# Expert weights of a hybrid block as 2 MB transfers with 16 KB rows, and the contraction orders permuted to fit

## The reference

```
logits = xt @ w_router + b_router                       # 512 tokens, 32 experts
top_val, top_idx = lax.top_k(logits, 4)
gates = jax.nn.softmax(top_val, axis=-1)
...
gu = xb @ w_gate_up[e] + b_gate_up[e]                   # (1024) x (1024 x 2048)
gate = jnp.minimum(gu[:, :D_EXPERT], 7.0)
up = jnp.clip(gu[:, D_EXPERT:], -7.0, 7.0)
act = (up + 1.0) * gate * jax.nn.sigmoid(1.702 * gate)
yb = act @ w_down[e] + b_down[e]                        # (1024) x (1024 x 1024)
```

## Time and profile before

| | |
|---|---|
| median of 3 runs | 1363.3 us (1361.44 to 1363.33) |
| profiled execution, its own time | 1363.13 us |
| its span, first to last instruction | 1361.4 us |
| PE busy | 1264.2 us, 93% |
| DVE, ACT, POOL busy | 38%, 21%, 12% |
| DMA moved | 455.66 MB, mean 335 GB/s |
| ring<-in_w_gate_up_dram | 256 transfers of 1024 KB |
| ring<-in_w_down_dram | 128 transfers of 1024 KB |
| mean granted TensorE clock | 0.969 of full speed |

### The profile page before, as it was taken

One profiled execution on the slowest core, in us unless ns is written; L12 is line 12 of the kernel. 1 busy time (PEld: TensorE's weight loads), 2 busy tenths in 40 slices (PEclk: granted clock), 3 DMA queues, 4 the chain that ended last, 5 costly groups with the idle time before them and its releaser, 6 DMA issues.

```text
span 1361.4 us, 52741 instructions
## 1 busy us (share of the span) xinstructions
PE 1264.2 (93%) x21755; PEld 742.5 (55%) x21755; DVE 520.2 (38%) x1710; ACT 288.4 (21%) x500; POOL 162.0 (12%) x257
## 2 busy tenths in 40 slices
PE   8999999973998999999999999999999999998882
PEld 4546555431655656656555655555565556555451
DVE  6553233226333333333333333343333334332238
ACT  4521124041121221121122121112212212211112
POOL 4100320033010010100101010010100101000010
PEclk9999999985999999999999999999999999999896
DMA  7452151237299999999999999999999999999997
GB/s 238 143 194 91 32 197 46 114 148 302 77 417 418 406 418 406 418 397 418 404 405 417 399 417 408 417 406 417 409 418 403 417 398 404 417 417 418 417 421 282
DMA packets 96851, 455.66 MB, mean 335 GB/s; under 512 B 11033, under 2 KB 22986, under 8 KB 63466
## 3 DMA queue, kind: packets, MB, share of 16 engines
q1 hardware_dynamic: 92768, 445.69, 81.5%
q0 software_dynamic: 3888, 8.40, 1.7%
q10 hardware_dynamic: 90, 0.03, 0.0%
HBM read 432.52 MB, written 23.27 MB: 335 GB/s over the span
## 4 chain that ended last, share of the span: by engine, by line
PE 65%; DMA 30%; DVE 3%; issue 2%; SPq 0%; POOL 0%; ACT 0%; DVEq 0%; POOLq 0%; ACTq 0%
PE ps L1696 25%; DMA ring<-in_w_gate_up_dram 18%; PE ps L1717 12%; PE ps L1309 11%; DMA ring<-in_w_down_dram 10%; PE ps L1658 5%; PE ps L1329 4%; PE ps L1376 1%; DMA x_rows_dram<-cat,rowi 1%; PE ps L1689 1%; PE ps L1708 1%; PE ps L1667 1%; PE ps L1369 1%; PE ps L1338 0%; DMA ring<-x_rows_dram 0%
## 5 line engine op out<-in xcount | busy, mean ns | idle before, releaser
L1696 PE MATMUL ps<-ring,cat 128*32 128x256 f32 x9856 | 557.7, 384 | 15.3 <-DMA ring<-in_w_gate_up_dram 15.3
L1696 PEld LDWEIGHTS ps<-ring,cat 128*32 128x32 f32 x9856 | 308.4, 111 | 236.0 <-DMA ring<-in_w_gate_up_dram 20.1
L1717 PE MATMUL ps<-ring,cat 128*32 128x256 f32 x4928 | 281.5, 379 | 3.9 <-DMA ring<-in_w_down_dram 3.0
L1717 PEld LDWEIGHTS ps<-ring,cat 128*32 128x32 f32 x4928 | 146.0, 110 | 110.5 <-DMA ring<-in_w_down_dram 7.5
L1309 PE MATMUL ps<-hbuf,ring 128*128 128x512 f32 x320 | 147.5, 607 | 0.4 <-DVE hbuf L846 0.4
L778 ACT ACTIVATE cat<-cat 128x128 f32<-128x128 f32 x154 | 47.7, 310 | 453.9 <-DVE cat L1239 453.9
L559 POOL DMA_INDIRECT pair_rows_dram<-cat,rowi x75 | 74.7, 996 | 505.1 <-ACT cat L782 505.1
L1221 DVE TENSOR_REDUCE wslot<-ps 128x2 f32<-128x6 f32 x77 | 12.7, 165 | 317.1 <-ACT cat L782 316.6
L782 ACT ACTIVATE cat<-ps,wslot 128x256 f32<-128x256 f32 x77 | 36.5, 474 | 367.7 <-PE ps L1717 363.0
L1658 PE MATMUL ps<-hbuf,cat 128*32 128x256 bf16 x2496 | 108.7, 274 | 3.7 <-DVE cat L1204 3.7
L1239 DVE TENSOR_SCALAR cat<-ps 128x128 f32<-128x128 f32 x154 | 44.9, 292 | 166.7 <-PE ps L1696 165.2
(11 more groups left out here) (308 smaller groups left out, 816.7 us busy)
## 6 DMA issues: line engine op xcount, KB each, us to landing
ring<-in_w_gate_up_dram SPq DMA_DIRECT2D x256, 1024.0 KB
ring<-in_w_down_dram SPq DMA_DIRECT2D x128, 1024.0 KB
ring<-in_w_in_dram SPq DMA_DIRECT2D x10, 1024.0 KB, 6.3
pair_rows_dram<-cat SPq DMA_DIRECT2D x4, 2048.0 KB, 11.0
ring<-pair_rows_dram SPq DMA_DIRECT2D x4, 2048.0 KB, 20.5
ring<-in_w_out_dram SPq DMA_DIRECT2D x1, 4096.0 KB, 12.9
ring<-in_x_dram SPq DMA_DIRECT2D x4, 512.0 KB, 5.4
x_rows_dram<-ring SPq DMA_DIRECT2D x1, 2048.0 KB, 16.9
```

The lines of the kernel that those rows point to most:

```text
L1696: last = mm(ps[SLOTS * q:SLOTS * (q + 1), gu_bank(half), 0:2 * P].rearrange("p (s j i) -> p s j i", s=2, j=4), xgT[:, SLOTS * u:SLOTS * (u ...
L1717: last = mm(ps[SLOTS * q:SLOTS * (q + 1), 1, 0:QD], actT[:, c // 4, SLOTS * (c % 4):SLOTS * (c % 4 + 1)], w[:, i, q * QD:(q + 1) * QD], st ...
```

## The change

The loads of `refill` are joined in pairs. Two neighbouring units, now "a pair", come with one transfer of 2 MiB in which each partition receives 16 KB from 16 KB that lie together in DRAM. For gate/up that is two neighbouring rows of 8 KB, for down four neighbouring rows of 4 KB. A partition therefore no longer holds row p of each chunk of 128, but rows 2p and 2p + 1 of 256 (gate/up), or 4p to 4p + 3 of 512 (down). The orders around it are changed to match:

- The first 20 units are still loaded one by one, but with the new row order (`unit_src`).
- Semaphores: one for a pair of slots. The first load of a pair counts 32 (two transfers), every later one 16 more (`pair_landed`).
- SP waits for both units of a pair to be used, and for the whole pair that holds unit n - 4. PE's `landed(u)` waits for the whole pair too.
- Gate/up contraction: `h2p` is written in the new column order by ACT's casts (`by_rows`, `natural`), and POOL's subtractions read it so.
- Down contraction: a quarter of the gate/up output is now 128 neighbouring columns instead of four groups of 32 (`quarter`), and DVE's last multiply writes its result in the order (j i) (`by_four`), so that the block transpose leaves row 4p + j on partition p.

```diff
         def quarter(v, q, half):
 
-            return v.rearrange("p s (j r) -> p s j r", r=P)[:, :, 4 * half:4 * half + 4, SLOTS * q:SLOTS * (q + 1)]
+            return v[:, :, 4 * P * half + P * q:4 * P * half + P * (q + 1)]
...
-        slot_in = [sem(f"slot_in{i}") for i in range(RING)]
+        slot_in = [sem(f"slot_in{i}") for i in range(RING // 2)]
...
             if u < NGU:
-                return w_gate_up[0, bass.ds(e, 1), u * P:(u + 1) * P, :].rearrange("a p c -> (a p) c")
+                rows = w_gate_up[0, bass.ds(e, 1), u // 2 * 2 * P:(u // 2 + 1) * 2 * P, :]
+                return rows.rearrange("a (p j) c -> p (a j) c", j=2)[:, u % 2, :]
             c = 2 * (u - NGU)
-            return w_down[0, bass.ds(e, 1), c * P:(c + 2) * P, :].rearrange("a (c p) n -> p (a c) n", c=2)
+            rows = w_down[0, bass.ds(e, 1), c // 4 * 4 * P:(c // 4 + 1) * 4 * P, :]
+            return rows.rearrange("a (p j) n -> p (a j) n", j=4)[:, c % 4:c % 4 + 2, :]
...
+        def pair_landed(turn):
+
+            return 32 + 16 * turn
...
+            def load_pair(e, u, slot):
+                c = 2 * (u - NGU)
+                if u < NGU:
+                    rows = w_gate_up[0, bass.ds(e, 1), u * P:(u + 2) * P, :].rearrange("a (p j) c -> p (a j c)", j=2)
+                else:
+                    rows = w_down[0, bass.ds(e, 1), c * P:(c + 4) * P, :].rearrange("a (p j) n -> p (a j n)", j=4)
+                pair = ring[:, slot * UNIT:(slot + 2) * UNIT]
+                sp.dma_start(pair, rows).then_inc(slot_in[slot // 2], 16)
...
-                for u in range(NU):
+                for u in range(0, NU, 2):
...
-                    sp.wait_ge(w_used, used + (u + 1))
-                    sp.wait_ge(slot_in[landed % RING], (landed // RING + 1) * 16)
-                    load_unit(following[n // NU - e], n % NU, n % RING)
+                    sp.wait_ge(w_used, used + (u + 2))
+                    sp.wait_ge(slot_in[landed % RING // 2], pair_landed(landed // RING))
+                    load_pair(following[n // NU - e], n % NU, n % RING)
...
-                G.tensor_tensor(h2[:, b, :], h2[:, b, :], h2p[0][:, b, :], ALU.subtract).then_inc(less_ok, 1)
+                G.tensor_tensor(natural(h2[:, b, :]), natural(h2[:, b, :]), by_rows(h2p[0][:, b, :]), ALU.subtract).then_inc(less_ok, 1)
...
-                A(h2p[0][:, b, :], h2[:, b, :], ACT.Copy).then_inc(h2p_ok, 1)
+                A(by_rows(h2p[0][:, b, :]), natural(h2[:, b, :]), ACT.Copy).then_inc(h2p_ok, 1)
...
-                    step(V.tensor_tensor(act_[:, half], uc[:, half], sg[:, half], ALU.mult), act_ok, n + 1)
+                    step(V.tensor_tensor(act_[:, half].rearrange("p (j i) -> p i j", j=4), by_four(uc[:, half]), by_four(sg[:, half]), ALU.mult), act_ok, n + 1)
...
                 def landed(u):
                     slot, turn = slot_of(e, u)
-                    pe.wait_ge(slot_in[slot], (turn + 1) * 16)
+                    pe.wait_ge(slot_in[slot // 2], pair_landed(turn))
```

More of the change, by code:

```diff
@@ L212, in gu_bank, with by_four, by_rows, natural @@
             return (0, 3)[half]
+        def by_four(v):
+            return v.rearrange("p (i j) -> p i j", j=4)
+        def by_rows(v):
+            return v.rearrange("p (v j r) -> p v r j", j=2, r=P)
+        def natural(v):
+            return v.rearrange("p (v r j) -> p v r j", j=2, r=P)
         def quarter(v, q, half):
-            return v.rearrange("p s (j r) -> p s j r", r=P)[:, :, 4 * half:4 * half + 4, SLOTS * q:SLOTS * (q + 1)]
+            return v[:, :, 4 * P * half + P * q:4 * P * half + P * (q + 1)]
         def bc(v, n, at):
@@ L342, in load_unit @@
             def load_unit(e, u, slot):
-                sp.dma_start(unit_dst(slot, u), unit_src(e, u)).then_inc(slot_in[slot], 16)
+                sp.dma_start(unit_dst(slot, u), unit_src(e, u)).then_inc(slot_in[slot // 2], 16)
+            def load_pair(e, u, slot):
[6 more added lines that the diff above has]
+                sp.dma_start(pair, rows).then_inc(slot_in[slot // 2], 16)
             load_unit(0, 0, 0)
@@ L520, in _ @@
                 pool.wait_ge(h2p_ok, b + 1)
-                G.tensor_tensor(h2[:, b, :], h2[:, b, :], h2p[0][:, b, :], ALU.subtract).then_inc(less_ok, 1)
+                G.tensor_tensor(natural(h2[:, b, :]), natural(h2[:, b, :]), by_rows(h2p[0][:, b, :]), ALU.subtract).then_inc(less_ok, 1)
             for b in range(TB):
                 pool.wait_ge(h2p_ok, TB + b + 1)
-                G.tensor_tensor(h2[:, b, :], h2[:, b, :], h2p[1][:, b, :], ALU.subtract).then_inc(less_ok, 1)
+                G.tensor_tensor(natural(h2[:, b, :]), natural(h2[:, b, :]), by_rows(h2p[1][:, b, :]), ALU.subtract).then_inc(less_ok, 1)
             def over_choices(weights, out):
@@ L762, in _ @@
                 act.wait_ge(less_ok, b + 1)
-                A(h2p[1][:, b, :], h2[:, b, :], ACT.Copy).then_inc(h2p_ok, 1)
+                A(by_rows(h2p[1][:, b, :]), natural(h2[:, b, :]), ACT.Copy).then_inc(h2p_ok, 1)
             act.wait_ge(top_ok, 1)
@@ L767, in _ @@
                 act.wait_ge(less_ok, TB + b + 1)
-                A(h2p[2][:, b, :], h2[:, b, :], ACT.Copy).then_inc(h2p_ok, 1)
+                A(by_rows(h2p[2][:, b, :]), natural(h2[:, b, :]), ACT.Copy).then_inc(h2p_ok, 1)
             act.wait_ge(tab_ok, 1)
@@ L1688, in expert_block @@
                     for q in range(Q):
-                        last = mm(ps[SLOTS * q:SLOTS * (q + 1), gu_bank(half), 0:2 * P].rearrange(
-                            "p (s j i) -> p s j i", s=2, j=4), selu[:, :], quarter(bias, q, half), start=True, stop=False)
+                        last = mm(ps[SLOTS * q:SLOTS * (q + 1), gu_bank(half), 0:2 * P].rearrange("p (s c) -> p s c", s=2), selu[:, :], quarter(bias, q, half), start=True, stop=False)
                 last.then_inc(gub_used, 1)
@@ L1695, in expert_block @@
                         for q in range(Q):
-                            last = mm(ps[SLOTS * q:SLOTS * (q + 1), gu_bank(half), 0:2 * P].rearrange(
-                                "p (s j i) -> p s j i", s=2, j=4), xgT[:, SLOTS * u:SLOTS * (u + 1)],
+                            last = mm(ps[SLOTS * q:SLOTS * (q + 1), gu_bank(half), 0:2 * P].rearrange("p (s c) -> p s c", s=2), xgT[:, SLOTS * u:SLOTS * (u + 1)],
                                 quarter(w, q, half), start=False, stop=u == NGU - 1)
```

## The result

The change makes the kernel slower: median 1390.2 us (1386.45 to 1393.55, 4 runs) against 1362.4 us in the same session, ratio 1.0205 with a 95% interval of 1.0176 to 1.0235. The forecast was 1358.0 us, with a range of 1352 to 1371 and 0.19 for slower. The profiled execution of after took 1393.55 us, with a span of 1391.8 us; the one of before had 1361.4. So 30.4 us of span are to be found, where the medians differ by 27.9: the profiled execution is the slowest of the four, 3.3 us over their median.

The account below looks back on a forecast made before the run. PE and transfers were taken as nearly balanced, PE slower by a hair in the middle. Late -4.3 and early -1.1 us, the rest nothing, made -5.4 on 1363.1: 1357.7, rounded to 1358 us, range 1352 to 1371.

Parts of the forecast that it names:

- Start: ACT's casts and POOL's subtractions ahead of the router and expert stage: stepped access costs 0, bounds 0 and +4 us.
- The subtractions on POOL: POOL's eight subtractions of some 2.1 us before the expert stage: may grow by 1 us each unseen; taken as 0.
- The rate: Weight loads: 16 KB rows take 2.46 us for a MiB, saving 1.05 us an expert, 0.087 us for each unit.
- Middle: Middle of the expert stage, where PE bounds: no gain taken, between -2 and +11 us.
- rival A: Expert stage: pair waits without the better rate, PE waiting up to 0.87 us every two experts; up to 1376; chance 0.17.
- Late and early: First blocks where PE waits for weights, last experts and fourth expert: faster loads give net -4.3 and -1.1 us.
- PE's own work: PE's gate/up read loses its runs of 32 columns: 0.43 us for four tiles stays, cost nothing.
- SwiGLU: DVE's multiply writing with a step: even twice its 0.29 us hides before the down product needs it.
- scatter: Scatter packets behind larger ones: median 6.1 us becomes 7 to 8, against a block of 12.3; cost nothing.

Follow-up runs that it names:

- cast_order: The change with casts and subtractions walked in another order, so that 2-byte writes are contiguous and 4-byte reads step by 8 bytes; 1366.4 us, ratio 1.0038.
- sp_pair_issue: `order_only` with SP alone waiting for whole pairs, then issuing two 1 MiB loads, PE waiting for single units; 1361.7 us, ratio 1.0000.
- pe_wait_alone: `order_only` with PE waiting for a pair by one wait, SP issuing single loads with 4 or 5 MiB in flight; 1363.0 us, ratio 1.0011.
- pairs_ahead6: `cast_order` with 6 MiB in flight instead of 4; 1360.4 us, ratio 0.9989.
- order_only: The change with single 1 MiB loads and unit waits, casts as in `cast_order`; only the permuted orders are left; 1358.4 us, ratio 0.9972.
- pe_pair_waits: `order_only` with PE alone waiting for both units of a pair, by two wait instructions; 1377.1 us, ratio 1.0128.

## Why the prediction was wrong, step by step

*Start: the step that failed.* It is this step that puts the time out of the range. With the casts in order the rest of the change took 1366.4 us, inside 1352 to 1371; that it is inside is luck, since it loses by the pair waits where the forecast had a gain. The step bounded the cost between 0 and 4 us and took 0; it was 22 to 24. Two things went wrong. The size: the text admitted that "no row shows a 2-byte write with a step", and then made a bound of a doubling, for which no row stood either. It was 4.5 times, not 2. The row it leaned on instead, L760 in the earlier trace rows, writes 4-byte elements in runs of 128, which says nothing about single 2-byte elements 256 bytes apart. The place: only the four first casts were counted as standing ahead of something that matters. The four middle casts and the Exp behind them had 7.2 us of idle ACT time as cover (0.16, 1.03 and 6.00 us in ACT's rows of before). At 4.7 us for each cast that cover was gone, and the softmax waited for eight casts. Even the doubling that the text named would have come to 8 x 1.05 = 8.4 us against these 7.2, had all eight been counted.

The subtractions on POOL did as the forecast allowed: 2.63 us each, where they took 2.1 to 2.2, hidden now behind the slow casts (their rows end "<-ACT hbuf"). The Trainium skill (GPSIMD Engine Reference, "Performance pitfalls for Q7 kernels") has half as much again for reads with such a step. The trace has a fifth: 2636 ns in after against 2212 in `cast_order` and 2209 before, with the long step on one of the two inputs.

*The rate.* Mis-sized. The term was 2.46 us for a MiB of 16 KB rows, 0.087 us saved for each unit. The median packet confirms it (611 ns for 615), the mean does not: at 636 ns a MiB costs 2.54 us, and an expert 12 x 2.54 = 30.5 us against the 30.6 of the sum. A sample of 4 us without a slow packet in it gave the median of what follows and hid its tail.

*Middle.* The step took 0 and kept +11 us as a bound by rival A. Rival A's mechanism happened, at the units it named: unit 10 is held for unit 11, 9.9 us of PE waits in 9 places where before had 0.2. Its condition did not hold as stated. It was to decide once a pair took over 5.1 us of engine time; the mean packet gives 8 x 0.636 = 5.09. What the runs point to is what the step left out: with 4 MiB in flight as only two transfers, SP too waits for whole pairs. `sp_pair_issue` and `pe_wait_alone` give the halves (0.3% and 0.4%), `pairs_ahead6` shows that depth takes most of it away (1.0038 to 0.9989, where `order_only` has 0.9972).

*Late and early.* Forecast -4.3 and -1.1 us. The early first block lasts 17.82 us, where it was 17.77: nothing gained. The four late ones last 19.86, 18.41, 17.98 and 17.82 us, 74.1 against 72.6. One of them, PE in order of time in after:

```profile
1240.64 2.77 PE L1722 MATMUL ps<-ring,cat 128*32 128x256 f32 x48
1245.89 4.52 PE L1722 MATMUL ps<-ring,cat 128*32 128x256 f32 x80 [2.48 <-DMA ring<-in_w_gate_up_dram]
1252.53 2.17 PE L1742 MATMUL ps<-ring,cat 128*32 128x256 f32 x32 [0.40 <-DMA ring<-in_w_down_dram]
1257.42 3.12 PE L1742 MATMUL ps<-ring,cat 128*32 128x256 f32 x32 [2.72 <-DMA ring<-in_w_down_dram]
1260.28 0.69 PE L1716 MATMUL ps<-cat,selu 96*32 96x256 bf16 x8
```

The waits stand at even units as forecast, though at 8 (0.40 us) beside 6 and 10; the pair's price was right in kind, the rate that was to pay for it was missing.

*PE's own work, SwiGLU, scatter.* Right. A gate/up part is 6.98 us in the chain (6.91 in the earlier trace rows) and PE's busy time over the whole span is unchanged. DVE's multiply takes 387 ns instead of 292, hidden. The scatter's wait on POOL grew (its longest from 6.6 to 8.1 us) and bound nothing.

*Did a gain exist?* Yes, 0.28% in `order_only`, where the forecast did not look for it most: by the row order alone, which makes 8 KB rows of down, without pairs. The three parts as the runs have them: about 3 us gained by the row order, 8 to 10 lost by the pairs, 22 to 24 lost by the casts.

What stays open: why the packets of the first down load of an expert take longest (in every kernel, the one before too), which no run varied by itself; from what step on a cast slows, of which only 256 bytes was run; and whether the two pair waits cost more together than their sum.

## What to carry to other kernels

When a layout is permuted, look at the order in which each instruction walks it: let the narrow writes be contiguous and put the step on the wide reads, and price each such instruction times its count ahead of the first consumer, not by its neighbour. When loads are joined, count the depth of the queue in transfers as well as in bytes, and count the wait for the second half on both sides, at the consumer and at the issuer. Where two engines are in balance, a price of nothing for a wait needs a row that shows slack; here there was none.

## What the runs showed of the hardware that was not expected

- ACT writes 1024 bfloat16 elements for each partition in 1.05 us in order, in 4.7 to 5.0 us with a step of 256 bytes, and in 1.13 us in order when it reads float32 with a step of 8 bytes.
- Median packets of 4, 8 and 16 KB take 159, 312 and 611 ns: from 8 to 16 KB only 2% a byte are to be gained, 1% beside the 309 ns of the 8 KB packets in `order_only`.
- Slow packets (over 800 ns for 16 KB, up to 2.6 us) gather in the first down load of each expert: 304 of the 589 in `cast_order` from 450 to 1200 us, 219 of 268 in `pairs_ahead6`. Where only gate/up has 16 KB packets hardly any is slow (mean 615 ns).
- PE's wait for a pair has the ratio 1.0128 as two wait instructions (`pe_pair_waits`) and 1.0011 as one (`pe_wait_alone`, which differs also by up to one more load in flight): with the second instruction PE stands idle for 12.3 us in 13 places from 450 to 1190 us that no transfer ends, and why stays open.
